# A Fourier stage whose sequence transform is split by parity and folded about the middle

## The chip, the cores and the metric

The kernel runs on one core of a Trainium2 chip. The metric is device time in microseconds (us) of one execution; the median over the runs shown is what is compared.

## What is computed

A two-layer transformer block in float32 on 512 tokens of 1024 features: a first block (projections, a bidirectional gated delta scan, a Fourier branch, gates, a mixture of 32 experts) and two plain attention layers. The change touches the Fourier branch alone. Of the projected input it takes 512 columns, in 4 groups of 128, and mixes each group over both axes:

```python
def fourier_mix(f):
    B, L, _ = f.shape
    fg = f.astype(jnp.float32).reshape(B, L, F_GROUPS, F_GROUP_DIM)
    return jnp.fft.fftn(fg, axes=(1, 3), norm='ortho').real.reshape(B, L, F_DIM).astype(f.dtype)
```

With f[l, d] for one group, the result at sequence position n and feature e is the sum over l and d of f[l, d] times (cos a cos b - sin a sin b), where a is the feature angle 2 pi d e / 128 and b the sequence angle 2 pi l n / 512. So it needs a cosine and a sine transform over the features, and then a cosine and a sine transform over the sequence, subtracted. The result is multiplied by `w_fourier_out` in the next stage.

## The kernel before

The program is a chain of stages. A stage opens a block with one instruction stream for each engine (TensorE, ScalarE, VectorE, GpSimd, and SyncE for the DMA queue); the streams wait for each other by semaphores, and each runs in its written order. All engines meet at a barrier at the end of a stage. PSUM is one tensor `g.PS` of 8 banks of 128 partitions x 512 floats.

`fourier_stage` (L1544 to L1640) is the stage that changes. The scan stage is ahead of it and the linear stage `ya` behind it, which multiplies the result by `w_fourier_out`. What each stream of the Fourier stage does, in order:

- **SyncE** loads the weights of the four groups (`W`, 512 KB each, L1565), the feature table `CS` (L1566: cosines and sines of 128 x 128), the sequence table `CL` (L1567: cosines and minus sines of 512 x 512, 2 MB), then the first pieces of the next stage's weights into a ring (L255) and some rows of biases (L1570), and waits for these rows.
- **TensorE** first projects: for each group 24 products of 128x512 with operands of the type fp32r (8 blocks of the contraction, each as hi x hi, lo x hi, hi x lo; the helper's lines L71 to L73), giving the group with features on partitions and 512 positions along the bank, in banks 0 to 3. Then the feature transform (L1586): for each pair of groups and each of four blocks of 128 positions, two plain float32 products of 128x256 (a block of positions as the stationary operand, `CS` as the moving one). Then the sequence transform (L1596): for each group, 8 plain float32 products of 128x512 that accumulate in one bank: 4 blocks of positions, cosine and sine. A plain float32 product is run as two passes, so the trace shows twice as many instructions as the code has products.
- **ScalarE** rounds the weights to the hi part (L1604), squares the scan's output `o` (L1608) and takes a root (L1610), both for a normalisation of `o` that has nothing to do with the transform, copies the projected groups out of PSUM to `fT` (L1614), copies half of the feature transform's results to `G` (L1617), and at last rounds each group's result to `FT.hi` (L1620). `G` lies in the memory of `W`.
- **VectorE** makes the low parts of the weights (L1626), sums the squares (L1629), inverts the root (L1631), scales `o` by it (L1634, four blocks), copies the other half of the feature transform (L1637), and makes `FT.lo` (L1640).

The order of the work is the written order of the streams; no planner is involved. Nothing is staggered across the groups: all four are projected, then all are transformed over the features, then all over the sequence. `ScalarE` and `VectorE` of the stage `ya` begin with the splits of its first weights (L646, L671), TensorE with its first product (L71).

`shape_tables` makes the tables on the host.

Of the kernel before, what the change touches and what calls it, by code (L numbers as in the profile page):

```python
# [15 lines left out]
P = 128  # L16
# [1526 lines left out]

def fourier_stage(nc, g, w_in, dft_feat, dft_seq, uT, FT, following, o, rows):  # L1544


    with Stage(nc, "fft", ["cs", "cl", "rows", "hi", "lo", "mm", "f", "g", "ga", "gd", "o", "oh", "sq", "ss", "rt", "rc"], [("w", NG)]) as st:
# [4 lines left out]
        CL = st.sb("CL", [P, NT, 2, SEQ])  # L1552
        fT = st.sb("fT", [P, NG, SEQ])
# [4 lines left out]
        G = W[:, :, :, :].rearrange("p g k n -> p (g k n)").rearrange("p (t g n) -> p t g n", t=NT, g=NG)  # L1558
        blk = st.block()

        @blk.sync
        def _(sp):
            wv = w_in.rearrange("(p k) n -> p k n", k=KD)
            for gr in range(NG):
                sp.dma_start(W[:, gr], wv[:, :, F_OFF + gr * P:F_OFF + (gr + 1) * P]).then_inc(s["w"][gr], 16)  # L1565
            sp.dma_start(CS[:, :], dft_feat).then_inc(s["cs"], 16)  # L1566
            sp.dma_start(CL[:, :, :, :], dft_seq.rearrange("(t p) c n -> p t c n", p=P)).then_inc(s["cl"], 16)  # L1567
            following.begin(sp, g.ring)
            for dst, src in rows:
                sp.dma_start(dst, src).then_inc(s["rows"], 16)  # L1570
            sp.wait_ge(s["rows"], 16 * len(rows))

        @blk.tensor
        def _(pe):
            for gr in range(NG):
                pe.wait_ge(s["lo"], gr + 1)
                for k in range(KD):
                    last = matmul3(nc, g.PS[:, gr, :], WP[:, gr, k, :], uT[:, k, :], k == 0, k == KD - 1)
                last.then_inc(s["mm"], 1)
            pe.wait_ge(s["cs"], 16)  # L1580
            for h in range(2):
                pe.wait_ge(s["f"], 2 * h + 2)
                for t in range(NT):
                    bank = (2, 3, 6, 7)[t] if h else (0, 1, 4, 5)[t]
                    for q in range(2):
                        last = nc.tensor.matmul(g.PS[:, bank, q * 256:(q + 1) * 256], fT[:, 2 * h + q, t * P:(t + 1) * P], CS[:, :], start=True, stop=True)  # L1586
                    last.then_inc(s["g"], 1)
            pe.wait_ge(s["cl"], 16)
            for gr in range(NG):
                if gr == 0:  # L1590
                    pe.wait_ge(s["ga"], NT)
                if gr == 2:
                    pe.wait_ge(s["gd"], NT)
                for t in range(NT):
                    for q in range(2):
                        last = nc.tensor.matmul(g.PS[:, gr, :], G[:, t, gr, q * P:(q + 1) * P], CL[:, t, q, :],  # L1596
                                                start=t == 0 and q == 0, stop=t == NT - 1 and q == 1)
                last.then_inc(s["o"], 1)

        @blk.scalar  # L1600
        def _(act):
            for gr in range(NG):
# [6 lines left out]
            act.wait_ge(s["ss"], NT)  # L1609
            nc.scalar.activation(rt[:, :, :], ss[:, :, :], ACT.Sqrt, bias=g.eps[:, 0:1], scale=1.0 / DH).then_inc(s["rt"], 1)  # L1610
            act.wait_ge(s["lo"], NG)
            for gr in range(NG):
                act.wait_ge(s["mm"], gr + 1)
                nc.scalar.copy(fT[:, gr, :], g.PS[:, gr, :]).then_inc(s["f"], 1)  # L1614
            for t in range(NT):
                act.wait_ge(s["g"], t + 1)
                nc.scalar.copy(G[:, t, 0:2, :], g.PS[:, (0, 1, 4, 5)[t], :].rearrange("p (g n) -> p g n", g=2)).then_inc(s["ga"], 1)  # L1617
            for gr in range(NG):
                act.wait_ge(s["o"], gr + 1)
                nc.scalar.copy(FT.hi[:, gr, :], g.PS[:, gr, :]).then_inc(s["oh"], 1)  # L1620

        @blk.vector
        def _(dve):
            for gr in range(NG):
                dve.wait_ge(s["hi"], gr + 1)
                nc.vector.tensor_tensor(WP.lo[:, gr], W[:, gr], WP.hi[:, gr].bitcast(F32), ALU.subtract).then_inc(s["lo"], 1)  # L1626
            for t in range(NT):
# [5 lines left out]
            for t in range(NT):  # L1633
                nc.vector.tensor_tensor(o[:, t], o[:, t], rc[:, t, :, None].to_broadcast([P, NV, DH]), ALU.mult)  # L1634
            for t in range(NT):
                dve.wait_ge(s["g"], NT + t + 1)
                nc.vector.tensor_copy(G[:, t, 2:4, :], g.PS[:, (2, 3, 6, 7)[t], :].rearrange("p (g n) -> p g n", g=2)).then_inc(s["gd"], 1)  # L1637
            for gr in range(NG):
                dve.wait_ge(s["oh"], gr + 1)
                nc.vector.tensor_tensor(FT.lo[:, gr, :], g.PS[:, gr, :], FT.hi[:, gr, :].bitcast(F32), ALU.subtract)  # L1640
# [97 lines left out]
def shape_tables():  # L1738
# [15 lines left out]
    j = np.arange(SEQ)  # L1754
    b = 2 * np.pi * ((j[:, None] * j[None, :]) % SEQ) / SEQ
    scale = 1.0 / np.sqrt(SEQ * P)
    seq = (np.stack([np.cos(b), -np.sin(b)], axis=1) * scale).astype(np.float32)
# [1550 lines left out]
```

## Time and profile before

| | us |
|---|---|
| median of 3 runs | 3851.17 (3850.42 to 3853.6) |
| profiled execution, its span from first to last instruction | 3851.9 |
| TensorE busy in it | 3515.4 (91%) |
| VectorE busy | 2738.6 (71%) |
| ScalarE busy | 1965.5 (51%) |
| GpSimd busy | 704.3 (18%) |

The profiled execution has no time of its own beside its span; the span is 0.7 us above the median of the runs. Engines overlap, so the busy times don't add up. The Fourier stage lies between about 704 and 771 us from the span's start. In the rows below, PE is TensorE's products, PEld its loads of stationary operands (they overlap PE), DVE VectorE, ACT ScalarE, POOL GpSimd. "128x512 f32" is partitions x elements; an idle time stands before the instruction that ended it, with the engine that released it. PEclk is the clock granted to TensorE, as a share of 2.4 GHz: 1.00 is 2.4 GHz, 0.50 is 1.2 GHz. Products are pipelined, so that the duration of one (592 ns) is longer than the distance between two starts.

### The profile page before, as it was taken

How to read it: one execution, taken by the hardware profiler on the slowest of the kernel's cores; microseconds unless marked ns; L12 is line 12 of the kernel's file. 1: busy time of each engine (PE TensorE's matmuls, PEld its weight loads, DVE VectorE, ACT ScalarE, POOL GpSimd, SP SyncE). 2: the span in 40 equal slices, each digit the busy share in tenths (PEclk: the TensorE clock that was granted, in tenths of full speed). 3: DMA queues.
4: the chain of work that ended last, by engine and by line, in shares of the span. 5: the costliest groups of instructions: out<-in, count | busy, mean ns of one | idle time of the engine just before them, and what ended most of it. 6: DMA issues, size and time to landing. Idle time of an engine off the chain costs nothing. (4 is left out here: it accounts for less than half of the span.)

```text
span 3851.9 us, 48477 instructions
## 1 busy us (share of the span) xinstructions
PE 3515.4 (91%) x17884; PEld 2912.3 (76%) x17884; DVE 2738.6 (71%) x3103; ACT 1965.5 (51%) x2530; POOL 704.3 (18%) x605
## 2 busy tenths in 40 slices
PE   4979999999969999999999997788899988879998
PEld 3768999677748888888888884667688767768876
DVE  5777777376569999999999996877676245753323
ACT  4533434223148888888888884357222223742222
POOL 1017767000000110011011012066000012720000
PEclk8989999999979999999999998899899989999999
DMA  5326011365359999999999995611466222013321
GB/s 171 113 109 242 12 45 34 111 228 186 133 227 356 377 376 390 377 374 390 378 374 390 379 374 215 199 32 45 131 197 196 88 79 54 34 46 103 93 93 66
DMA packets 285349, 752.62 MB, mean 195 GB/s; under 512 B 35528, under 2 KB 161160, under 8 KB 232186
## 3 DMA queue, kind: packets, MB, share of 16 engines
q1 hardware_dynamic: 271820, 696.01, 50.0%
q0 software_dynamic: 8480, 36.71, 2.7%
q10 hardware_dynamic: 4896, 17.83, 1.1%
q8 instruction: 101, 1.65, 0.2%
q14 instruction: 52, 0.43, 0.0%
HBM read 698.97 MB, written 57.01 MB: 196 GB/s over the span
## 5 line engine op out<-in xcount | busy, mean ns | idle before, releaser
L2238 DVE TENSOR_TENSOR ex_WP_lo<-ex_W,ex_WP_hi 128x2048 fp32r<-128x2048 f32 x408 | 918.5, 2285 | 43.9 <-ACT ex_WP_hi L2162 42.6
L2162 ACT CAST ex_WP_hi<-ex_W 128x2048 fp32r<-128x2048 f32 x408 | 766.9, 1910 | 196.9 <-PE PS L73 159.8
L71 PE MATMUL PS<-ex_WP_hi,ex_xT_hi 128*128 128x512 f32 x1056 | 418.7, 396 | 11.0 <-DVE ex_xT_lo L2247 5.6
L73 PE MATMUL PS<-ex_WP_hi,ex_xT_lo 128*128 128x512 f32 x1056 | 412.5, 391 | 0.0
L72 PE MATMUL PS<-ex_WP_lo,ex_xT_hi 128*128 128x512 f32 x1056 | 412.1, 390 | 0.0
L2080 POOL COPY r_idc<-r_idx 128x1 uint32 x33 | 73.9, 2241 | 1044.5 <-PE PS L2093 1044.5
L71 PEld LDWEIGHTS PS<-ex_WP_hi,ex_xT_hi 128*128 128x128 f32 x1056 | 198.9, 188 | 64.1 <-issue 24.8
L71 PE MATMUL PS<-ex_WP_hi,ex_aT_hi 128*128 128x512 f32 x576 | 230.0, 399 | 10.1 <-DVE ex_aT_lo L2247 5.3
L73 PEld LDWEIGHTS PS<-ex_WP_hi,ex_xT_lo 128*128 128x128 f32 x1056 | 198.7, 188 | 42.2
L72 PEld LDWEIGHTS PS<-ex_WP_lo,ex_xT_hi 128*128 128x128 f32 x1056 | 199.0, 188 | 39.4
L73 PE MATMUL PS<-ex_WP_hi,ex_aT_lo 128*128 128x512 f32 x576 | 226.4, 393 | 0.0
L72 PE MATMUL PS<-ex_WP_lo,ex_aT_hi 128*128 128x512 f32 x576 | 226.0, 392 | 0.0
L2743 POOL TENSOR_SCALAR lpj<-lpj 128x512 f32<-128x512 f32 (+2 forms) x128 | 176.2, 1387 | 50.5 <-DVE lpj L2905 50.1
L71 PE MATMUL PS<-lhT_hi,fu_WP_hi 128*128 128x512 f32 x464 | 181.7, 392 | 0.1
L73 PE MATMUL PS<-lhT_hi,fu_WP_lo 128*128 128x512 f32 x464 | 180.9, 390 | 0.0
L72 PE MATMUL PS<-lhT_lo,fu_WP_hi 128*128 128x512 f32 x464 | 180.7, 389 | 0.0
L3124 DVE TENSOR_TENSOR fd_WP_lo<-ringb,fd_WP_hi 128x1024 fp32r<-128x1024 f32 x44 | 53.6, 1225 | 169.4 <-ACT fd_WP_hi L3115 169.4
L1395 ACT COPY sc_Pm<-PS 128x512 f32<-128x512 f32 x144 | 84.4, 586 | 154.9 <-PE PS L1320 154.0
L71 PE MATMUL PS<-fd_WP_hi,lha_hi 128*128 128x512 f32 x352 | 139.2, 395 | 11.6 <-DVE fd_WP_lo L3124 11.6
L72 PE MATMUL PS<-fd_WP_lo,lha_hi 128*128 128x512 f32 x352 | 138.6, 394 | 0.0
L73 PE MATMUL PS<-fd_WP_hi,lha_lo 128*128 128x512 f32 x352 | 138.4, 393 | 0.0
L3115 ACT CAST fd_WP_hi<-ringb 128x1024 fp32r<-128x1024 f32 x44 | 45.7, 1048 | 176.1 <-PE PS L73 173.2
(623 smaller groups left out, 8637.4 us busy)
## 6 DMA issues: line engine op xcount, KB each, us to landing
ex_W<-in_w_gate SPq DMA_DIRECT2D x136, 1024.0 KB, 7.3
ex_W<-in_w_up SPq DMA_DIRECT2D x136, 1024.0 KB, 7.8
ex_W<-in_w_down SPq DMA_DIRECT2D x136, 1024.0 KB, 8.2
ringb<-in_w_gu SPq DMA_DIRECT2D x88, 512.0 KB, 4.1
ringb<-in_w_mod SPq DMA_DIRECT2D x72, 512.0 KB, 4.6
ringa<-in_w_mod SPq DMA_DIRECT2D x56, 512.0 KB, 4.8
s_ybuf<-x_sb SPq DMA_DIRECT2D x3, 8192.0 KB, 27.1
ringb<-in_w_down SPq DMA_DIRECT2D x44, 512.0 KB, 3.5
```

Of the source, the lines that this page charges most:

```text
L71: nc.tensor.matmul(out, lhs.hi, rhs.hi, start=start, stop=False)
L72: nc.tensor.matmul(out, lhs.hi, rhs.lo, start=False, stop=False)
L73: return nc.tensor.matmul(out, lhs.lo, rhs.hi, start=False, stop=stop)
L1395: nc.scalar.copy(Pm[:, b], PS4[:, 2 * b, :, :]).then_inc(s["pm"], 1)
L2080: nc.gpsimd.tensor_copy(r.idc[:, 0:1], r.idx[:, bass.ds(j + 2, 1)]).then_inc(s["icp"], 1)
L2162: nc.scalar.copy(WP.hi[:, c % RP], W[:, c % RAW]).then_inc(s["hi"], 1)
L2238: nc.vector.tensor_tensor(WP.lo[:, c % RP], W[:, c % RAW], WP.hi[:, c % RP].bitcast(F32), ALU.subtract).then_inc(s["lo"][c % RP], 1)
L2743: nc.gpsimd.tensor_scalar(score(n - 1), score(n - 1), rd[:, n - 1:n], None, ALU.mult).then_inc(s["na"], 1)
L3115: nc.scalar.copy(WP.hi[:, m % RP], ring.slot(m, stream.sources[m])).then_inc(s["hi"], 1)
L3124: nc.vector.tensor_tensor(WP.lo[:, m % RP], ring.slot(m, stream.sources[m]), WP.hi[:, m % RP].bitcast(F32), ALU.subtract).then_inc(s["done ...
```

## The change

The sequence transform uses two symmetries of cosine and sine. First, position n of the output is even or odd. For even n the angle repeats after 256 positions of the input, so the two halves of the input are added; for odd n it changes its sign, so they are subtracted. Second, each half (256 positions) is symmetric or antisymmetric about its middle, so that position m and 256 - m are added or subtracted. What is left are four arrays of 128 positions for each group (`SUM_COS`, `DIF_SIN`, `SUM_SIN`, `DIF_COS`) and four tables of 128 x 256. The input at the middle of the sum half (`QUARTER`) takes the place of row 0 of the sine tables, which is zero: it is brought there by a product with a tile `middle` (one column filled, the rest zero), and the tables' row 0 holds +-1 instead.

By engine:

- TensorE, for each group: the same 24 products of the projection; 5 plain float32 products of 128x128 for the features (L1586's 4 of 128x256 go); 4 of 128x256 for the sequence (L1596's 8 of 128x512 go). The groups are staggered: project 0, project 1, features 0, project 2, features 1, sequence 0, project 3, features 2, sequence 1, features 3, sequence 2, sequence 3.
- ScalarE: the copy of a projected group takes 256 columns instead of 512 (`upper`); a copy of 512 columns for each group behind the features (`gather`; four before on ScalarE and four on VectorE, now four on ScalarE); `high` writes `FT.hi` at every second element, since the bank holds the even positions and then the odd ones. The wait for `lo` now stands ahead of the root.
- VectorE, for each group: `folds`, with an addition and a subtraction of 256 elements (PSUM and `half`), a wait for both, an addition and a subtraction of 2 x 127 elements with one operand read backwards, and three copies of 2, 1 and 1 elements; then the scaling of one block of `o`. Two memsets stand ahead of the sums (128x4 and 128x512). `low` reads and writes at every second element.
- SyncE: `CL` is 512 KB instead of 2 MB.

```diff
@@ -1541,22 +1541,30 @@
                 nc.vector.tensor_copy(place(n), g.PS[:, n % 8, :].rearrange("p (j n) -> p j n", n=P)).then_inc(s["dve"], 1)
+HALF_SEQ, QUARTER = SEQ // 2, SEQ // 4
+
+
 def fourier_stage(nc, g, w_in, dft_feat, dft_seq, uT, FT, following, o, rows):
-    with Stage(nc, "fft", ["cs", "cl", "rows", "hi", "lo", "mm", "f", "g", "ga", "gd", "o", "oh", "sq", "ss", "rt", "rc"], [("w", NG)]) as st:
+    with Stage(nc, "fft", ["cs", "cl", "rows", "hi", "lo", "mm", "half", "sg", "zero", "fold", "g", "ga", "o", "oh", "sq", "ss", "rt", "rc"], [("w", NG)]) as st:
         s = st.s
         W = st.sb("W", [P, NG, KD, P])
         WP = pair(st.sb, "WP", [P, NG, KD, P])
         CS = st.sb("CS", [P, 2 * P])
-        CL = st.sb("CL", [P, NT, 2, SEQ])
-        fT = st.sb("fT", [P, NG, SEQ])
+        CL = st.sb("CL", [P, 4, HALF_SEQ])
+        half = st.sb("half", [P, NG, HALF_SEQ])
+        sg = st.sb("sg", [P, NG, 2, HALF_SEQ])
+        middle = st.sb("middle", [P, NG, P])
         sq = st.sb("sq", [P, 2, NV, DH])
         ss = st.sb("ss", [P, NT, NV])
         rt = st.sb("rt", [P, NT, NV])
         rc = st.sb("rc", [P, NT, NV])
-        G = W[:, :, :, :].rearrange("p g k n -> p (g k n)").rearrange("p (t g n) -> p t g n", t=NT, g=NG)
+        flat = W[:, :, :, :].rearrange("p g k n -> p (g k n)")
+        fold, G = [flat[:, n * NG * 4 * P:(n + 1) * NG * 4 * P].rearrange("p (g a n) -> p g a n", g=NG, a=4) for n in range(2)]
         blk = st.block()
+        SUM_COS, DIF_SIN, SUM_SIN, DIF_COS = range(4)
+        FEAT = {SUM_COS: slice(0, P), DIF_COS: slice(0, P), SUM_SIN: slice(P, 2 * P), DIF_SIN: slice(P, 2 * P)}
 
         @blk.sync
         def _(sp):
@@ -1564,7 +1572,7 @@
             for gr in range(NG):
                 sp.dma_start(W[:, gr], wv[:, :, F_OFF + gr * P:F_OFF + (gr + 1) * P]).then_inc(s["w"][gr], 16)
             sp.dma_start(CS[:, :], dft_feat).then_inc(s["cs"], 16)
-            sp.dma_start(CL[:, :, :, :], dft_seq.rearrange("(t p) c n -> p t c n", p=P)).then_inc(s["cl"], 16)
+            sp.dma_start(CL[:, :, :], dft_seq).then_inc(s["cl"], 16)
 ...
@@ -1572,33 +1580,58 @@
 
         @blk.tensor
         def _(pe):
-            for gr in range(NG):
+            def project(gr):
                 pe.wait_ge(s["lo"], gr + 1)
                 for k in range(KD):
                     last = matmul3(nc, g.PS[:, gr, :], WP[:, gr, k, :], uT[:, k, :], k == 0, k == KD - 1)
                 last.then_inc(s["mm"], 1)
-            pe.wait_ge(s["cs"], 16)
-            for h in range(2):
-                pe.wait_ge(s["f"], 2 * h + 2)
-                for t in range(NT):
-                    bank = (2, 3, 6, 7)[t] if h else (0, 1, 4, 5)[t]
-                    for q in range(2):
-                        last = nc.tensor.matmul(g.PS[:, bank, q * 256:(q + 1) * 256], fT[:, 2 * h + q, t * P:(t + 1) * P], CS[:, :], start=True, stop=True)
-                    last.then_inc(s["g"], 1)
-            pe.wait_ge(s["cl"], 16)
-            for gr in range(NG):
+
+            def features(gr):
+                pe.wait_ge(s["fold"], gr + 1)
                 if gr == 0:
-                    pe.wait_ge(s["ga"], NT)
-                if gr == 2:
-                    pe.wait_ge(s["gd"], NT)
-                for t in range(NT):
-                    for q in range(2):
-                        last = nc.tensor.matmul(g.PS[:, gr, :], G[:, t, gr, q * P:(q + 1) * P], CL[:, t, q, :],
-                                                start=t == 0 and q == 0, stop=t == NT - 1 and q == 1)
+                    pe.wait_ge(s["cs"], 16)
+                for a in range(4):
+                    out = g.PS[:, 4 + gr, a * P:(a + 1) * P]
+                    last = nc.tensor.matmul(out, fold[:, gr, a, :], CS[:, FEAT[a]], start=True, stop=a != SUM_SIN)
+                    if a == SUM_SIN:
+                        last = nc.tensor.matmul(out, middle[:, gr, :], CS[:, FEAT[SUM_COS]], start=False, stop=True)
+                last.then_inc(s["g"], 1)
+
+            def sequence(gr):
+                pe.wait_ge(s["ga"], gr + 1)
+                if gr == 0:
+                    pe.wait_ge(s["cl"], 16)
+                for parity, arrays in enumerate(((SUM_COS, SUM_SIN), (DIF_COS, DIF_SIN))):
+                    for n, a in enumerate(arrays):
+                        last = nc.tensor.matmul(g.PS[:, gr, parity * HALF_SEQ:(parity + 1) * HALF_SEQ], G[:, gr, a, :], CL[:, 2 * parity + n, :],
+                                                start=n == 0, stop=n == 1)
                 last.then_inc(s["o"], 1)
+            project(0)
+            project(1)
+            features(0)
+            project(2)
+            features(1)
+            sequence(0)
+            project(3)
+            features(2)
+            sequence(1)
+            features(3)
+            sequence(2)
+            sequence(3)
 
         @blk.scalar
         def _(act):
+            def upper(gr):
+                act.wait_ge(s["mm"], gr + 1)
+                nc.scalar.copy(half[:, gr, :], g.PS[:, gr, HALF_SEQ:SEQ]).then_inc(s["half"], 1)
+
+            def gather(gr):
+                act.wait_ge(s["g"], gr + 1)
+                nc.scalar.copy(G[:, gr], g.PS[:, 4 + gr, :].rearrange("p (a n) -> p a n", n=P)).then_inc(s["ga"], 1)
+
+            def high(gr):
+                act.wait_ge(s["o"], gr + 1)
+                nc.scalar.copy(FT.hi[:, gr, :].rearrange("p (m e) -> p e m", e=2), g.PS[:, gr, :].rearrange("p (e m) -> p e m", e=2)).then_inc(s["oh"], 1)
 ...
@@ -1607,37 +1640,59 @@
                     act.wait_ge(s["ss"], t - 1)
                 nc.scalar.activation(sq[:, t % 2], o[:, t], ACT.Square).then_inc(s["sq"], 1)
             act.wait_ge(s["ss"], NT)
+            act.wait_ge(s["lo"], NG)
             nc.scalar.activation(rt[:, :, :], ss[:, :, :], ACT.Sqrt, bias=g.eps[:, 0:1], scale=1.0 / DH).then_inc(s["rt"], 1)
-            act.wait_ge(s["lo"], NG)
-            for gr in range(NG):
-                act.wait_ge(s["mm"], gr + 1)
-                nc.scalar.copy(fT[:, gr, :], g.PS[:, gr, :]).then_inc(s["f"], 1)
-            for t in range(NT):
-                act.wait_ge(s["g"], t + 1)
-                nc.scalar.copy(G[:, t, 0:2, :], g.PS[:, (0, 1, 4, 5)[t], :].rearrange("p (g n) -> p g n", g=2)).then_inc(s["ga"], 1)
-            for gr in range(NG):
-                act.wait_ge(s["o"], gr + 1)
-                nc.scalar.copy(FT.hi[:, gr, :], g.PS[:, gr, :]).then_inc(s["oh"], 1)
+            upper(0)
+            upper(1)
+            gather(0)
+            upper(2)
+            gather(1)
+            high(0)
+            upper(3)
+            gather(2)
+            high(1)
+            gather(3)
+            high(2)
+            high(3)
 
         @blk.vector
         def _(dve):
+            def folds(gr):
+                dve.wait_ge(s["half"], gr + 1)
+                nc.vector.tensor_tensor(sg[:, gr, 0, :], g.PS[:, gr, 0:HALF_SEQ], half[:, gr, :], ALU.add).then_inc(s["sg"], 1)
+                nc.vector.tensor_tensor(sg[:, gr, 1, :], g.PS[:, gr, 0:HALF_SEQ], half[:, gr, :], ALU.subtract).then_inc(s["sg"], 1)
+                dve.wait_ge(s["sg"], 2 * gr + 2)
+                front, back = sg[:, gr, :, 1:P], sg[:, gr, :, HALF_SEQ - 1:P:-1]
+                nc.vector.tensor_tensor(fold[:, gr, 0:2, 1:P], front, back, ALU.add)
+                nc.vector.tensor_tensor(fold[:, gr, 2:4, 1:P], front, back, ALU.subtract)
+                nc.vector.tensor_copy(fold[:, gr, 0::3, 0], sg[:, gr, :, 0])
+                nc.vector.tensor_copy(middle[:, gr, 0:1], sg[:, gr, 0, QUARTER:QUARTER + 1])
+                nc.vector.tensor_copy(fold[:, gr, 1, 0:1], sg[:, gr, 1, QUARTER:QUARTER + 1]).then_inc(s["fold"], 1)
+
+            def low(gr):
+                dve.wait_ge(s["oh"], gr + 1)
+                nc.vector.tensor_tensor(FT.lo[:, gr, :].rearrange("p (m e) -> p e m", e=2), g.PS[:, gr, :].rearrange("p (e m) -> p e m", e=2),
+                                        FT.hi[:, gr, :].rearrange("p (m e) -> p e m", e=2).bitcast(F32), ALU.subtract)
             for gr in range(NG):
                 dve.wait_ge(s["hi"], gr + 1)
                 nc.vector.tensor_tensor(WP.lo[:, gr], W[:, gr], WP.hi[:, gr].bitcast(F32), ALU.subtract).then_inc(s["lo"], 1)
+            dve.wait_ge(s["lo"], NG)
+            nc.vector.memset(fold[:, :, SUM_SIN, 0:1], 0.0).then_inc(s["zero"], 1)
+            nc.vector.memset(middle[:, :, :], 0.0).then_inc(s["zero"], 1)
             for t in range(NT):
                 dve.wait_ge(s["sq"], t + 1)
                 nc.vector.reduce_sum(ss[:, t, :], sq[:, t % 2], AX.X).then_inc(s["ss"], 1)
             dve.wait_ge(s["rt"], 1)
             nc.vector.reciprocal(rc[:, :, :], rt[:, :, :]).then_inc(s["rc"], 1)
             dve.wait_ge(s["rc"], 1)
-            for t in range(NT):
-                nc.vector.tensor_tensor(o[:, t], o[:, t], rc[:, t, :, None].to_broadcast([P, NV, DH]), ALU.mult)
-            for t in range(NT):
-                dve.wait_ge(s["g"], NT + t + 1)
-                nc.vector.tensor_copy(G[:, t, 2:4, :], g.PS[:, (2, 3, 6, 7)[t], :].rearrange("p (g n) -> p g n", g=2)).then_inc(s["gd"], 1)
+            dve.wait_ge(s["zero"], 2)
             for gr in range(NG):
-                dve.wait_ge(s["oh"], gr + 1)
-                nc.vector.tensor_tensor(FT.lo[:, gr, :], g.PS[:, gr, :], FT.hi[:, gr, :].bitcast(F32), ALU.subtract)
+                folds(gr)
+                nc.vector.tensor_tensor(o[:, gr], o[:, gr], rc[:, gr, :, None].to_broadcast([P, NV, DH]), ALU.mult)
+                if gr == 3:
+                    low(0)
+            for gr in range(1, NG):
+                low(gr)
 def first_half(nc, g, I, C, scratch):
@@ -1751,10 +1806,14 @@
         selrow[r, r, :] = 1.0
     a = 2 * np.pi * ((i[:, None] * i[None, :]) % P) / P
     feat = np.concatenate([np.cos(a), np.sin(a)], axis=1).astype(np.float32)
-    j = np.arange(SEQ)
-    b = 2 * np.pi * ((j[:, None] * j[None, :]) % SEQ) / SEQ
+    m = np.arange(HALF_SEQ)
     scale = 1.0 / np.sqrt(SEQ * P)
-    seq = (np.stack([np.cos(b), -np.sin(b)], axis=1) * scale).astype(np.float32)
+    even = 2 * np.pi * ((2 * i[:, None] * m[None, :]) % SEQ) / SEQ
+    odd = 2 * np.pi * ((i[:, None] * (2 * m[None, :] + 1)) % SEQ) / SEQ
+    turns = 1.0 - 2.0 * (m % 2)
+    even_sin, odd_sin = -np.sin(even), -np.sin(odd)
+    even_sin[0], odd_sin[0] = turns, -turns
+    seq = (np.stack([np.cos(even), even_sin, np.cos(odd), odd_sin], axis=1) * scale).astype(np.float32)
     return {"t_ident": ident, "t_cum": cum, "t_levels": lev, "t_selrow": selrow, "t_dft_feat": feat, "t_dft_seq": seq}
 
 
```

## Rows read from the trace of the kernel before

**Rows 1.** the windows view (stretch: us, busy us of each engine with instructions, clock, DMA)

```profile
707.00:713.70 6.70, 2.65 (x6) 2.15 (x7) 2.77 (x3) 3.13 (x3) 0.00 (x0) 0.52 1.19 305
713.70:724.00 10.30, 10.30 (x45) 8.29 (x44) 9.29 (x9) 7.26 (x9) 0.00 (x0) 0.98 1.04 396
724.00:741.60 17.60, 17.60 (x80) 14.66 (x79) 4.27 (x6) 4.00 (x7) 0.00 (x0) 1.00 0.32 125
741.60:769.50 27.90, 27.83 (x66) 12.14 (x64) 2.99 (x5) 1.79 (x4) 0.00 (x0) 1.00 0.00 1
...
772.00:778.80 6.80, 4.90 (x12) 3.83 (x13) 5.47 (x4) 3.43 (x4) 3.33 (x2) 0.51 0.92 324
```

**Rows 2.** groups by line on TensorE, 703 to 790 (busy us, mean ns)

```profile
L1596 PE MATMUL PS<-fft_CL,fft_W 128*128 128x512 f32 x64 | 27.6, 592 | 0.0
...
L1586 PE MATMUL PS<-fft_CS,fft_fT 128*128 128x256 f32 x32 | 7.1, 379 | 0.0
```

**Rows 3.** the waits, 734 to 771.5 (us in total, times, longest)

```profile
ACT FT_hi L1620 <- PE PS L1596: 28.6, 4, 9.7
```

**Rows 4.** the timeline of ScalarE, 716 to 739 (start us, us, idle before)

```profile
721.06 0.32 ACT L1610 ACTIVATE fft_rt<-fft_ss,eps 128x32 f32<-128x32 f32 x1
...
723.89 0.59 ACT L1614 COPY fft_fT<-PS 128x512 f32<-128x512 f32 x1 [2.04 <-PE PS L73]
...
735.09 0.59 ACT L1614 COPY fft_fT<-PS 128x512 f32<-128x512 f32 x1 [5.01 <-PE PS L73]
735.96 0.59 ACT L1617 COPY fft_W<-PS 128x512 f32<-128x512 f32 x1 [0.28 <-PE PS L1586]
736.82 0.59 ACT L1617 COPY fft_W<-PS 128x512 f32<-128x512 f32 x1 [0.28 <-PE PS L1586]
```

**Rows 5.** the timeline of TensorE: last scan products, then the sequence products

```profile
698.66 1.06 PE L1371 MATMUL PS<-sc_T,ktok 128*128 128x128 f32 x8
...
741.80 27.63 PE L1596 MATMUL PS<-fft_CL,fft_W 128*128 128x512 f32 x64
```

**Rows 6.** the timeline of VectorE, 716 to 726.6

```profile
716.31 4.68 DVE L1629 TENSOR_REDUCE fft_ss<-fft_sq 128x8 f32<-128x1024 f32 x4
721.41 0.35 DVE L1631 RECIPROCAL fft_rc<-fft_rt 128x32 f32<-128x32 f32 x1 [0.41 <-ACT fft_rt L1610]
721.80 4.63 DVE L1634 TENSOR_TENSOR x_sb<-x_sb,fft_rc 128x1024 f32<-128x1024 f32 x4
```

**Rows 7.** the timeline at the stage's end and the next stage's start

```profile
769.47 0.59 ACT L1620 CAST FT_hi<-PS 128x512 fp32r<-128x512 f32 x1 [6.28 <-PE PS L1596]
770.08 0.69 DVE L1640 TENSOR_TENSOR FT_lo<-PS,FT_hi 128x512 fp32r<-128x512 f32 x1 [6.18 <-ACT FT_hi L1620]
...
773.90 0.80 PE L71 MATMUL PS<-ya_WP_hi,FT_hi 128*128 128x512 f32 x1 [4.47 <-DVE ya_WP_lo L671]
```

**Rows 8.** one line at a time (ns min/median/max): prices of small steps

```profile
L1434 DVE TENSOR_TENSOR sc_B<-sc_B,PS x32: 380/405/411, 436.2 to 652.4; 128x256 f32<-128x256 f32 x32
...
L1002 ACT COPY qkv_padc<-PS x16: 372/374/378, 90.7 to 244.8; 128x256 f32<-128x256 f32 x16
...
L2266 DVE MEMSET ex_bp<- x1: 912/912/912, 1101.0 to 1101.0; 128x1024 f32 x1
...
L2905 DVE RECIPROCAL lpj<-lpj x128: 148/158/165, 2562.5 to 3387.1; 128x1 f32<-128x1 f32 x128
```

**Rows 9.** the line L379, strided (yb) and unstrided (mo) reads

```profile
L379 DVE SCALAR_TENSOR_TENSOR yb_bacc<-ringa,silu,yb_bacc x7: 2112/2211/2293, 952.8 to 972.4; 128x1024 f32<-128x1024 f32 x7
L379 DVE SCALAR_TENSOR_TENSOR mo_bacc<-ringa,silu,mo_bacc x7: 1283/1284/1285, 1010.9 to 1029.4; 128x1024 f32<-128x1024 f32 x7
```

**Rows 10.** a TensorE wait in the scan, and the windows around it

```profile
606.25 1.53 PE L1298 MATMUL PS<-ident,sc_L 128*128 128x128 f32 x12 [1.64 <-DVE sc_L L1426]
...
606.00:609.50 3.50, 3.25 (x29) 3.25 (x30) 0.88 (x2) 0.00 (x0) 1.83 (x2) 1.00 0.00 0
609.50:620.00 10.50, 10.50 (x97) 10.50 (x96) 6.43 (x10) 4.40 (x8) 7.24 (x6) 1.00 0.01 2
```

## The prediction

> **What bounds the kernel now.** I read the windows view first, over the Fourier stage. From 713.7 to 769.5 us TensorE is busy all the time (10.30 of 10.30, 17.60 of 17.60, 27.83 of 27.90 us) while VectorE is busy 2.99 us of the last 27.90 and ScalarE less, and the DMA share there is 0.00 [rows 1]. Who works in that last stretch is told by the groups by line: 64 passes of L1596, the sequence transform, are the 27.6 us; the feature transform is 32 passes of L1586 [rows 2]. The waits show the other side: ScalarE waits 28.6 us in all for the four sequence results, and VectorE stands behind it [rows 3]. So what ends last is TensorE, and what it does longest is what the change cuts. The stage's exit is a chain of three: last product, the rounding of FT.hi (0.59 us), FT.lo (0.69 us), then the barrier and the next stage [rows 7].
>
> **What is removed.** The duration of a product includes its drain, so I use distances. 64 passes of 128x512 take 27.63 us and the last alone 0.59, so 63 distances are 27.04 us, 0.429 us each [rows 5]; 64 x 0.429 = 27.5 us. For 128x256, ScalarE's copies of feature results start 0.86 us apart (735.96 and 736.82) with four passes between them, 0.215 us each [rows 4]; 32 x 0.215 = 6.9 us. Together 34.4 us leave TensorE. The loads of stationary operands hide beside either, or the distance would not halve with the columns.
>
> **What is added on TensorE.** Features: 5 products x 2 passes x 4 groups = 40 passes of 128x128. In the scan, which has this size alone, 97 passes start in 10.50 us of unbroken work, 0.108 us each; and a run of twelve takes 1.53 us where a run of eight takes 1.06, 0.118 each [rows 5, 10]. I take 0.112: 40 x 0.112 = 4.5 us. Sequence: 4 x 2 x 4 = 32 passes of 128x256, 32 x 0.215 = 6.9 us. The projection keeps its 96 products; a group takes 5.60 us at full clock (ScalarE is released by group 1 at 723.89 and by group 3 at 735.09 [rows 4]). Net on TensorE: 34.4 - 11.4 = 23.0 us less.
>
> **Whether TensorE now waits.** The new order is worth following in time, since the folds stand on VectorE between a projection and its features.
>
> Group 0 is projected at about 723.85 - 5.60 = 718.25 us, group 1 at 723.85. But VectorE is late: the four sums run from 716.31 to 720.99, the root on ScalarE ends at 721.38, the reciprocal at 721.76 [rows 4, 6]. The two memsets come ahead of the sums. One of 1024 elements took 0.91 us [rows 8], so I take 0.5 us for 512, and 0.55 with the small one; the sums are back to back, so all behind them moves by 0.55: reciprocal done at 722.3. `upper(0)` stands behind the root on ScalarE, 721.85 to 722.2 (0.37 us for 256 columns [rows 8]). Folds(0) begin at 722.3: two operations of 256 elements at 0.40, two of 254 at the same, three tiny ones at 0.16 each (the one-element reciprocal took 158 ns) [rows 8], in all 2.1 us: 724.4. Features(0) could begin at 723.85, so there is a new wait of 0.6 us, 0.7 with the restart. Queued behind it on TensorE is project(2); nobody else waits. If the memsets cost nothing the wait is 0.1 us; if the folds take twice as long it is 2.8 us.
>
> From there, TensorE: features(0) to 725.7, project(2) 731.3, features(1) 732.4, sequence(0) 734.1, project(3) 739.7, features(2) 740.8, sequence(1) 742.6, features(3) 743.7, sequence(2) 745.4, sequence(3) 747.1. What each needs: fold(1) comes behind one scaling of `o` (1.22 us, 4.63 us for four [rows 6]) at 727.8, in time for 731.3; fold(2) at about 733.9 for 739.7; fold(3) is the tight one: upper(3) ends at 740.15, fold(3) at 742.3, 0.3 us before TensorE asks. Gather(3) (0.59 us for 512 columns [rows 4]) ends at 744.4, for 745.4. The four scalings, 4.6 us, fill VectorE's gaps; the scaling behind folds(3) holds low(0) to low(2), which still end before high(3). ScalarE has high(0) ahead of upper(3), but it ends at 734.8. So no second wait; the exit (0.59 + 0.69 us) is as before.
>
> **DMA.** `CL` moves 1.5 MB less and the pieces behind it land earlier. Worth nothing: in the trace of before the DMA share is 0.00 from 741.6 on and TensorE never waited for `CL` [rows 1]; the new stage's end (748.4) is still behind the last of the old traffic (0.32 share between 724 and 741.6, none after). The copies out of PSUM that VectorE loses (L1637) were off the path. The next stage's start, 3.1 us from FT.lo's end to its first product [rows 7], is the same work.
>
> **The sum.** -34.4 + 11.4 + 0.7 = -22.3 us. Against the profiled execution's own 3851.9 us that is 3829.6; against the median of the runs, 0.7 us lower, 3828.9. I put 3829.
>
> **Unknown prices.** (a) Writing and reading every second element. The nearest row is L379, which reads every eighth: 2.21 us against 1.28 for 1024 elements, 0.9 ns an element more [rows 9]. By it high(3) and low(3) would be 0.45 to 0.9 us longer each, 1.4 us in all; the other end is nothing. I take nothing: a step of two is far nearer to the row without a step than to the one with a step of eight. The Trainium skill's page "SBUF — State Buffer", section "Door 1: The DMA port swizzle", states that accesses within a 16-byte line run at full bandwidth, so that float32 may be strided up to 4 elements for free; by it the cost is zero, and L379's rows, beyond that step, agree. (b) The backward read. No row shows one. Below: 0.40 us as forward; above: L379's rate, 254 x 0.9 ns = 0.23 us more for each of two; a gain has no mechanism. I take 0.40. Both ends make fold(3) 0.45 us later, about its slack, and the first wait 0.45 us longer. (c) The memset, 0 to 0.9 us, taken 0.55. (d) TensorE's clock, as a rival.
>
> **Rivals.**
> 1. *VectorE becomes the bound of the tail.* If folds cost twice the 2.1 us (strides, drains at the wait within a fold), features(0) waits 2.1 us more and features(3) 1.8 us; with strided exits 1.4 us: 22.3 - 5.3 = 17 us, so 3834. For it: the slack at fold(3) is only 0.3 us. Against: the 256-element rows are tight, 380 to 411 ns.
> 2. *The clock dips once.* TensorE's clock falls to half after it stands still between stages (0.52 in 707 to 713.7, 0.51 in 772 to 778.8 [rows 1]). A dip of that length (6.8 us) at the new wait would cost half of it, 3.4 us: 3832. Against: in the scan TensorE waited 1.64 us, with 1.00 before, in and behind it [rows 10].
> 3. *Slower: the clock stays low.* The new order cycles through banks 0 to 7 with waits between short groups. If the clock fell to 1.2 GHz at features(0) and stayed there, the 22.6 us of TensorE work left in this stage would take 45.2, which by itself brings the time back to 3852; if it lasts through the next stage too, whose 96 products at 5.60/24 = 0.233 us are 22.4 us, another 19 us (3.4 us of them are paid in the dip that is there already) make it about 3871. It decides from the point where the low clock covers 30 us of work: 22.3 + 7.7. The Trainium skill's page "TensorE: Matmul & The Clock Gate", section "A second HAM failure mode: psum-queue depth-cycling", warns of just that: small idle times between groups of products while banks are cycled make the clock swing. The trace of before speaks against it: the scan runs small products with such waits at 1.00 [rows 10].
> 4. *The gain is not there*, since passes of 256 columns would be bound by their loads. But L1586's passes are of that very size with a load each, and are 0.215 us apart, half the distance of the 512-column ones; and the scan's 128-column passes, each with its load too, are half as far apart again [rows 4, 10]. Nearly excluded. Were each feature pass as far apart as one of 256 columns, 40 x 0.103 = 4.1 us would go: 3833.
>
> **How the numbers follow.** A measurement of this kernel can tell about 0.2%, 7.7 us, from no change. The forecast (3825 to 3831.5, that is its bounds and 2 us of scatter, about what the runs of before show) has 0.78; rival 1 has 0.11, rival 2 0.05, rival 4 0.02; rival 3 0.02, half of it ending near no change and half slower; something unnamed near no change 0.02. Faster needs under 3843.5: 0.96. Same 0.03, slower 0.01. The range: downwards no wait at all (3828.2) less scatter, and a low-clock stretch behind the stage that may fall otherwise against the shifted work (up to 3 us either way): 3824. Upwards it takes in rivals 1 and 2: 3836.
>
> **What would show it.** In the profile after: the stage's last FT.lo 22 us earlier, at about 748; sequence passes 32 of 128x256 and feature passes 40 of 128x128 with distances of 0.215 and 0.112 us; one wait of TensorE of 0.5 to 1 us for fold(0) and none for fold(3); clock 1.00 from 714 to the stage's end; everything behind shifted and otherwise the same. Wrong would be: a second wait for fold(3) or gather(3), a VectorE operation with a backward operand of 0.6 us or more, FT.hi of over 1 us, or a clock of 0.50 within the stage.

## The result and the profile after

| | before | after |
|---|---|---|
| median, us | 3851.32 (3850.42 to 3853.6, 4 runs) | 3828.68 (3826.51 to 3829.87, 4 runs) |
| profiled execution | 3851.9 | 3825.7 |
| first product of the Fourier stage to the end of its last FT.lo ("stage length") | 59.73 | 37.80 |

The ratio is 0.994 (95% interval 0.9927 to 0.9953): 22.6 us faster, where 3829 us and 22.3 us were forecast. The two profiled executions differ by 26.2 us, the stage by 21.9 of them. The rest isn't the change's as far as the profiles tell: 1.3 us of it lie ahead of the stage, and a second profile of the kernel before (below) is 2.8 us shorter than the first, which leaves 23.4. Where both the time and the span of one execution are known, the span is 1.8 to 2.3 us the shorter (3825.7 of 3827.75 after). So the execution profiled before took about 3854 us, an estimate, which is above the three runs of before. Its span of 3851.9 us should not be set beside their median, as the forecast and the part ahead of it do with the 0.7 us.

The windows view of the stage after, cut where the clock rises (stretch: us, busy us of TensorE, its loads, VectorE, ScalarE, GpSimd, clock, DMA):

```profile
709.73:715.10 5.37, 5.37 (x13) 4.21 (x14) 3.67 (x3) 3.87 (x5) 0.00 (x0) 0.50 1.11 346
715.10:747.53 32.43, 31.07 (x157) 26.09 (x155) 19.38 (x43) 10.58 (x17) 0.00 (x0) 1.00 0.29 111
```

In the second stretch TensorE is busy 31.07 of 32.43 us, and the 1.36 us left are about its exit, the time of FT.hi and FT.lo [rows 7]. So it is never stopped, and once the stage has begun the waits view shows no wait of TensorE in it. The clock was low for 5.37 us of the stage; before, for 3.0 us (711.04 to 714.0). At half clock that costs half its length. Without it the stage is 59.73 - 1.48 = 58.25 us before and 37.80 - 2.69 = 35.11 after: 23.1 us less, where the passes on TensorE were put at 23.0.

TensorE's timeline after, features(0), sequence(1), features(3), sequence(2) and (3):

```profile
723.45 0.83 PE L1595 MATMUL PS<-fft_CS,fft_W 128*128 128x128 f32 x6
...
739.70 1.89 PE L1606 MATMUL PS<-fft_CL,fft_W 128*128 128x256 f32 x8
741.43 0.83 PE L1595 MATMUL PS<-fft_CS,fft_W 128*128 128x128 f32 x6
742.10 0.39 PE L1597 MATMUL PS<-fft_CS,fft_middle 128*128 128x128 f32 x2
742.32 0.39 PE L1595 MATMUL PS<-fft_CS,fft_W 128*128 128x128 f32 x2
742.55 3.62 PE L1606 MATMUL PS<-fft_CL,fft_W 128*128 128x256 f32 x16
```

Features(0) has no idle time ahead of it. Features(3) and what follows give the distances: 741.43 to 742.55 for ten passes of 128x128, 0.112 us each, and 739.70 to 741.43 for eight of 128x256, 0.216 each. These are the rows that answer to [rows 5] and to the distances out of [rows 4].

VectorE's timeline after, from the second memset to the last tiny copy of folds(0), the last one of folds(3), and the last FT.lo:

```profile
715.27 0.48 DVE L1681 MEMSET fft_middle<- 128x512 f32 x1
715.67 4.63 DVE L1684 TENSOR_REDUCE fft_ss<-fft_sq 128x8 f32<-128x1024 f32 x4
720.71 0.35 DVE L1686 RECIPROCAL fft_rc<-fft_rt 128x32 f32<-128x32 f32 x1 [0.41 <-ACT fft_rt L1644]
721.10 0.42 DVE L1662 TENSOR_TENSOR fft_sg<-PS,fft_half 128x256 f32<-128x256 f32 x1
721.44 0.41 DVE L1663 TENSOR_TENSOR fft_sg<-PS,fft_half 128x256 f32<-128x256 f32 x1
721.89 0.42 DVE L1666 TENSOR_TENSOR fft_W<-fft_sg 128x254 f32<-128x254 f32 x1
722.23 0.42 DVE L1667 TENSOR_TENSOR fft_W<-fft_sg 128x254 f32<-128x254 f32 x1
722.57 0.16 DVE L1668 COPY fft_W<-fft_sg 128x2 f32<-128x2 f32 x1
...
722.70 0.14 DVE L1670 COPY fft_W<-fft_sg 128x1 f32<-128x1 f32 x1
...
740.79 0.14 DVE L1670 COPY fft_W<-fft_sg 128x1 f32<-128x1 f32 x1
...
746.84 0.69 DVE L1674 TENSOR_TENSOR FT_lo<-PS,FT_hi 128x512 fp32r<-128x512 f32 x1 [1.02 <-ACT FT_hi L1634]
```

The operations with a backward operand (L1666, L1667) take 0.42 us, as the forward ones (L1662) do. Operations issued back to back start 0.34 us apart, 0.45 where a wait for both sums lies between (L1663 to L1666), the tiny ones 0.07: folds(0) run from 721.10 to 722.84, 1.74 us. FT.lo with every second element takes 0.69 us, as in [rows 7].

ScalarE's timeline, a gather and the last two roundings:

```profile
739.90 0.59 ACT L1630 COPY fft_W<-PS 128x512 f32<-128x512 f32 x1 [0.74 <-PE PS L1595]
...
744.48 0.62 ACT L1634 CAST FT_hi<-PS 128x512 fp32r<-128x512 f32 x1 [1.14 <-PE PS L1606]
746.20 0.61 ACT L1634 CAST FT_hi<-PS 128x512 fp32r<-128x512 f32 x1 [1.11 <-PE PS L1606]
```

And TensorE's, the next stage's first product:

```profile
750.68 0.80 PE L71 MATMUL PS<-ya_WP_hi,FT_hi 128*128 128x512 f32 x1 [4.52 <-DVE ya_WP_lo L671]
```

FT.hi with every second element takes 0.61 to 0.64 us against 0.59 [rows 7]. The wait at the stage's exit is as before: 3.15 us from the end of FT.lo to the next product, against 3.13.

### The profile page after: what moved, and what is told of

Its sections match the earlier page's. It is cut to its first block and busy times, and to the rows that moved or that the text cites. A ratio compares the mean times of both kernels' runs of the same rounds, so it can differ in the third digit from the quotient of the medians.

```text
span 3825.7 us, 48456 instructions
## 1 busy us (share of the span) xinstructions
PE 3491.9 (91%) x17860; PEld 2906.4 (76%) x17860; DVE 2741.4 (72%) x3129; ACT 1965.4 (51%) x2530; POOL 703.6 (18%) x605
```

## Experiments

"Longer" and "shorter" are against the changed kernel, whose stage length is 37.80 us. Since medians scatter by 1 to 2 us, the stage length of the profile is named beside them.

**The changed kernel once more.**

> The changed kernel once more, as the measure for the three kernels beside it. The stage length (first product of the Fourier stage to the end of its last FT.lo) was 59.7 us before and 37.8 us after, where TensorE's clock was low for 10.2 us at the stage's start instead of 6.8. Theory (TensorE alone sets the stage): median 3827 to 3831, stage length 36.1 to 37.8 by how long the low clock lasts, TensorE's wait for fold(0) 0 to 0.5 us, larger where the clock rises early. Rival (the profile after was lucky, and the fold chain shows in other executions): a wait of TensorE of over 1 us.

Measured: 3827.9 us (5 runs; before 3850.95), stage length 37.83 us, no wait of TensorE. A third time, beside the last experiment: 3826.45 us and 37.82 us.

**Parity without folding.** In features, `sg` itself is stationary, in blocks of 128 positions; the table has the positions 0 to 255 for either parity, 1 MB. The features of a group go to one of two pairs of banks, so that those of groups 2 and 3 also wait for a gather.

```diff
-                    out = g.PS[:, 4 + gr, a * P:(a + 1) * P]
-                    last = nc.tensor.matmul(out, fold[:, gr, a, :], CS[:, FEAT[a]], start=True, stop=a != SUM_SIN)
...
+                    h, b = divmod(a, 2)
+                    last = nc.tensor.matmul(banks[:, gr % 2, a * 2 * P:(a + 1) * 2 * P], sg[:, gr, h, b * P:(b + 1) * P], CS[:, :], start=True, stop=True)
...
+                    for n in range(4):
+                        b, q = divmod(n, 2)
+                        last = nc.tensor.matmul(g.PS[:, gr, parity * HALF_SEQ:(parity + 1) * HALF_SEQ], G[:, gr, 2 * parity + b, q * P:(q + 1) * P],
+                                                CL[:, 4 * parity + n, :], start=n == 0, stop=n == 3)
```

> The split by parity without the folding about the middle: for each group 4 feature products of 128x256 instead of 5 of 128x128, and 8 sequence products of 128x256 instead of 4; VectorE has only the two operations of 256 elements, no memsets. The staggered order is kept. Theory (each pass costs its distance on TensorE): sequence 64 x 0.215 = 13.8, features 32 x 0.215 = 6.9, in all 20.7 us against 11.4, so 9.3 us longer than the changed kernel and 13.7 shorter than before: about 3838. Rival (the gain came from the staggering, or VectorE's folds bound the stage, so that their absence pays back the passes): within 3 us of the changed kernel.

Measured: 3838.98 us, ratio to before 0.9968 (0.9956 to 0.998); stage length 47.13 us, 9.3 longer, as forecast to the tenth. TensorE's timeline of it:

```profile
740.95 1.89 PE L1597 MATMUL PS<-fft_CS,fft_sg 128*128 128x256 f32 x8
742.68 3.62 PE L1607 MATMUL PS<-fft_CL,fft_W 128*128 128x256 f32 x16
746.13 1.89 PE L1597 MATMUL PS<-fft_CS,fft_sg 128*128 128x256 f32 x8
747.86 7.07 PE L1607 MATMUL PS<-fft_CL,fft_W 128*128 128x256 f32 x32
```

Eight feature passes, then sixteen sequence passes, all 0.216 us apart. So of the gain in passes the split by parity gives 13.7 us (58.25 less 44.48, the stage lengths before and here without the time lost at the low clock) and the folding 9.3, and VectorE's folds take nothing of it back.

**Not staggered.** TensorE runs `project` for the four groups, then `features`, then `sequence`; ScalarE `upper`, `gather`, `high` likewise.

```diff
-            project(0)
-            project(1)
-            features(0)
...
+            for step in (project, features, sequence):
+                for gr in range(NG):
+                    step(gr)
```

> All products of the changed kernel, but not staggered: project all four, features of all four, sequence of all four, and ScalarE's steps likewise. Theory (only the number of passes counts; three groups' features, 3.4 us, cover the 2.4 us of upper(3) and folds(3), and features(1) to (3) cover the gathers): within 0.5 us of the changed kernel, no wait of TensorE over 0.3 us. Rival (the staggering is what hides folds and gathers): 2.4 us or more longer, with a wait of TensorE ahead of features(3) or sequence(0).

Measured: 3827.58 us (ratio to before 0.9939, 0.9925 to 0.9952), stage length 37.97 us. TensorE's timeline:

```profile
735.61 0.83 PE L1595 MATMUL PS<-fft_CS,fft_W 128*128 128x128 f32 x6
...
740.07 7.07 PE L1606 MATMUL PS<-fft_CL,fft_W 128*128 128x256 f32 x32
```

From 735.61 on it never stops. The staggering as such is worth nothing. What matters is that other work of TensorE's lies between a group's projection and its features, and this order has that too.

**One group behind the other.** In this order nothing lies between. ScalarE takes `upper`, `gather`, `high` group by group too, and VectorE makes FT.lo of a group before the next group's folds.

```diff
-            project(0)
-            project(1)
-            features(0)
...
+            for gr in range(NG):
+                project(gr)
+                features(gr)
+                sequence(gr)
```

> All products of the changed kernel, one group wholly behind the other: project, features, sequence of group 0, then of group 1, and so on; nothing covers folds and gathers. Theory: TensorE waits for fold(0) about 4.9 us (it is done with group 0 at about 717.9, the fold at 722.8), for the three other folds 2.3 us each, for the four gathers 0.9 us each: 15.4 us longer than the changed kernel, plus 3.4 us for the clock, which falls at the first wait as it did at the wait of 3.57 us in the run with the scalings first; about 3847, and the shorter waits leave the clock at 1.00. Rival (the order of the groups is worth nothing, as the run without the stagger could be read): within 2 us of the changed kernel. Second rival (many short waits also lower the clock): over 3851.

Measured: 3853.55 us, ratio to before 1.0007 (0.9997 to 1.0016): the whole gain is gone. Stage length 61.88 us, 24.1 longer. The waits of TensorE in it (us in total, times, longest):

```profile
PE PS L1595 <- DVE fft_W L1654: 11.3, 4, 4.6
PE PS L1606 <- ACT fft_W L1622: 2.7, 4, 0.7
```

And the windows (columns as above):

```profile
724.20:731.00 6.80, 6.12 (x19) 5.14 (x20) 1.09 (x1) 0.61 (x2) 0.00 (x0) 0.53 0.22 86
731.00:737.00 6.00, 5.53 (x24) 4.13 (x22) 0.72 (x2) 0.98 (x2) 0.00 (x0) 1.00 0.00 0
...
741.00:745.00 4.00, 4.00 (x11) 3.23 (x12) 0.00 (x0) 0.48 (x1) 0.00 (x0) 0.60 0.00 0
745.00:751.00 6.00, 5.08 (x22) 3.76 (x20) 1.17 (x3) 0.52 (x2) 0.00 (x0) 1.00 0.00 0
751.00:758.00 7.00, 5.01 (x19) 4.11 (x20) 2.36 (x7) 0.59 (x1) 0.00 (x0) 0.76 0.00 0
```

The waits are 14.0 us, near the 15.4 expected. But the clock fell in each of the four groups: 0.53 over 6.8 us, then 0.60 over 4.0 and 0.76 over 7.0, and once more in the last. All low stretches in the stage behind its start sum to 17.0 us. TensorE works in 15.9 of them, which loses 8.0 us. 14.0 + 8.0 = 22.0 of 24.1. About 1.8 more are an estimate from the rows: a wait is counted from the end of the last product's duration (0.40 or 0.39 us), but the next product would have started 0.23 or 0.11 us behind its start, so each of the eight waits costs 0.17 or 0.28 us more than it is shown with. The first theory said that the short waits would leave the clock alone; that fell, and the second rival's mechanism holds. It is that of the slower rival of the prediction, but the clock swung and did not stay low: the Trainium skill's page "TensorE: Matmul & The Clock Gate", section "A second HAM failure mode: psum-queue depth-cycling", says that small idle times between groups of products make the clock swing. In this order the trace agrees, with 8.0 us lost. The changed kernel has no such idle times, so it neither bears this out nor speaks against it.

**All scalings first**, which moves fold(0) behind them:

```diff
             for gr in range(NG):
+                nc.vector.tensor_tensor(o[:, gr], o[:, gr], rc[:, gr, :, None].to_broadcast([P, NV, DH]), ALU.mult)
+            for gr in range(NG):
                 folds(gr)
-                nc.vector.tensor_tensor(o[:, gr], o[:, gr], rc[:, gr, :, None].to_broadcast([P, NV, DH]), ALU.mult)
...
```

> The changed kernel with VectorE's four scalings of o ahead of all folds, as their place was before. Fold(0) is ready 4.6 us later, fold(1) 3.5 us later. Theory: TensorE, 0.6 us of slack in the profile after, waits about 4 us for fold(0), and everything behind moves by that: 4 us longer than the changed kernel, if the clock stays at 1.00; if so long a stand makes the clock fall for about 6.8 us as at the stage ends, 7.4 us longer. Rival (slack elsewhere takes the wait in, since the later folds have 3 us and more to spare): under 1.5 us longer.

Measured: 3834.44 us, 6.5 longer than the changed kernel's 3827.9; stage length 44.28 us, 6.5 longer. TensorE's timeline at the wait:

```profile
727.97 1.65 PE L1595 MATMUL PS<-fft_CS,fft_W 128*128 128x128 f32 x6 [3.57 <-DVE fft_W L1670]
```

And the windows (columns as above):

```profile
728.00:733.00 5.00, 5.00 (x17) 4.42 (x18) 1.52 (x7) 0.58 (x1) 0.00 (x0) 0.50 0.00 0
733.00:755.00 22.00, 20.20 (x105) 17.10 (x103) 6.10 (x18) 4.96 (x9) 0.00 (x0) 1.00 0.00 0
```

A wait of 3.57 us, and 1.2 GHz from 726.4 to 733.2 us, 5.2 us of it under work. The wait is paid in full, and the clock adds half of these 5.2 us, 2.6: together 6.2 of the 6.5 us. None of the later slack takes it in.

**Two scalings first**, the same edit for two of the four.

> The changed kernel with two of the four scalings of o ahead of folds(0): fold(0) 2.3 us later. With the slack of 0.6 us TensorE waits about 1.7 us. Theory: the time grows by that alone and the clock stays at 1.00, as in the scan's wait of 1.64 us: 1.7 us longer than the changed kernel. Rival: this wait too is followed by a low clock of 6.8 us: 5.1 us longer.

Measured: stage length 39.63 us, 1.8 longer; 3828.5 us, which scatter hides. TensorE's waits:

```profile
PE PS L1595 <- DVE fft_W L1670: 1.4, 1, 1.4
```

And the windows (columns as above):

```profile
724.00:730.00 6.00, 4.56 (x26) 3.70 (x25) 3.25 (x15) 0.96 (x2) 0.00 (x0) 1.00 0.14 55
730.00:750.00 20.00, 18.54 (x98) 15.79 (x96) 8.27 (x20) 5.01 (x9) 0.00 (x0) 1.00 0.00 0
```

1.4 us of standing still cost about their own length (1.8 us of stage length in all), with the clock at 1.00.

**The wide table.** `CL` holds the table three times (1.5 MB).

```diff
-        CL = st.sb("CL", [P, 4, HALF_SEQ])
+        CL = st.sb("CL", [P, 3 * 4, HALF_SEQ])
```

> The changed kernel with the sequence table loaded three times over, 1.5 MB instead of 512 KB (the last two thirds are not read). Theory (the saved traffic is worth nothing): no difference over 0.5 us in the stage length (37.8 us), no wait of TensorE. Rival (the shorter load is part of the gain): 2 us or more longer, with a wait for the table or for the pieces of the next stage.

Measured: 3828.82 us, stage length 38.02 us, no wait of TensorE. The extra 1 MB, two thirds of the saved traffic, costs at most 0.2 us; the last third was not put back.

**The memsets on GpSimd**, behind its own wait for `lo`.

> The changed kernel with its two memsets on GpSimd, which is idle in this stage. The folds begin about 0.55 us earlier. Theory: TensorE has slack there already, so the stage length stays at 37.8 us. Rival (fold(0) is what TensorE is released by): 0.5 us shorter.

Measured: one time of 3827.0 us, stage length 37.81 us. The folds begin 0.5 us earlier behind the stage's first product (10.88 against 11.37 us), and features(0) begins 13.72 us behind it in both. Fold(0) is not what releases TensorE.

**The kernel before, once more.**

> The kernel before once more, for its profile: in all profiles of the new variants the clock was low for 10.2 us around the stage's start, in the one of before for 6.8 us. Theory (chance of where the low stretch begins): 6.8 or 10.2 us, stage length 59.7 or 60.6 us; the stage length less the time lost at the low clock agrees with the first within 0.2 us. Rival (the change itself makes the low stretch longer): 6.8 us again with 59.7 us.

Measured: one time of 3851.37 us, span 3849.1. The windows of the part of the low stretch that lies in the stage, and of the one behind the stage (columns as above):

```profile
709.30:714.60 5.30, 5.30 (x13) 4.14 (x14) 3.62 (x4) 3.80 (x5) 0.00 (x0) 0.50 1.11 358
...
772.70:776.10 3.40, 2.88 (x7) 2.30 (x8) 3.40 (x4) 2.05 (x3) 1.52 (x1) 0.50 1.02 397
```

The low stretch lasts from 704.4 to 714.6 us, 10.2 us, with a stage length of 60.79 us. Less half of the 5.3 us of it that lie in the stage that is 58.14, beside 58.25 of the first profile. So the longer low stretch isn't the change's. Behind the stage the clock was low for 3.4 us here, and for 6.8 us (772.1 to 778.9) in the first profile.

**A step further: the next stage's first piece split ahead.** The tables and copies that shrank leave room for a tile in which GpSimd splits the first piece of `w_fourier_out`. The code below is the new stream alone; the tile is also made ahead of the stage and handed to the next one.

```diff
+        @blk.gpsimd
+        def _(pool):
+            ahead.split(pool, g.ring, following, 0, s["ah"])
```

> The changed kernel, and GpSimd, idle in this stage, splits the first piece of the next stage's weights (hi and low part) into a tile kept for it; the memory is what the smaller tables and copies set free. The next stage's first product then need not wait for ScalarE and VectorE: 3.15 us from FT.lo's end to it become about 1.3 us. Theory: 1.9 us shorter than the changed kernel; if TensorE then stands too briefly for the clock to fall behind the stage (a wait of 1.4 us left it at 1.00, one of 2.2 and one of 0.7 close together did not), up to 3.4 us more: 3823 to 3827. Rival (the next stage is held by VectorE's splits of the pieces behind the first anyway): no gain over 0.5 us.

Measured: 3824.72 us (3822.43 to 3829.6), 3.2 below the changed kernel's 3827.9, on another chip and not beside it. The timeline, from the last FT.lo to the next product:

```profile
746.20 0.69 DVE L1678 TENSOR_TENSOR FT_lo<-PS,FT_hi 128x512 fp32r<-128x512 f32 x1 [1.02 <-ACT FT_hi L1634]
...
747.71 0.47 PE L71 MATMUL PS<-firsta_hi,FT_hi 128*128 128x512 f32 x1 [2.19 <-PEq L116]
```

And the windows (columns as above):

```profile
748.60:752.00 3.40, 3.40 (x10) 2.63 (x9) 3.23 (x3) 2.03 (x3) 0.00 (x0) 0.50 0.98 298
752.00:760.00 8.00, 8.00 (x36) 6.51 (x36) 1.64 (x3) 0.59 (x1) 3.44 (x2) 1.00 0.67 269
```

The product starts 0.82 us behind FT.lo instead of 3.15, so 2.3 us of standing still are won at that place. The low clock lasts 3.4 us instead of 6.8, another 1.7 us. But that part can't be put down to the edit: the kernel before once more and the kernel with two scalings first, both with the usual wait at the exit, had 3.4 us there as well. On the whole kernel the gain did not show side by side:

> The changed kernel, beside the next one, for a comparison on one chip: 3827 to 3829 us, stage length 37.8 us (36.1 if the low clock ends early).

> The version with the next stage's first piece split by GpSimd, once more. Theory: its profile was 4.4 us shorter (2.3 us of the wait behind the stage, 1.7 us by a low clock of 3.4 instead of 6.8 us), and the medians of two submissions 3.2 us apart; side by side it is 2 to 5 us shorter than the changed kernel. Rival (the difference was scatter): within 1 us.

Measured: 3826.45 us for the changed kernel, 3827.33 with the split ahead (3825.04 to 3829.0); profiled spans 3824.4 and 3825.3. The local gain is there again (0.82 us, and a low clock of 3.4 us against 6.8), and at the start of the experts' stage the kernel is still 1.6 us ahead (1123.6 against 1125.2 us), behind a Fourier stage that began 1.7 us later. That the kernel is 2 to 5 us shorter, as expected, was not borne out; whether it gains at all is open. The medians are 0.9 us apart with ranges of 4 us and more, and the scatter of low-clock stretches may hide it, which is argued and not shown.

## Why the prediction was right

- **The bound and the sum of passes** were right: 34.4 us of passes out, 11.4 in, at distances measured after as 0.216 and 0.112 us; 23.0 forecast, 23.1 found once the low clock is set aside. The profiles themselves differ by 21.9 in the stage, since the one after lost 1.2 us more there at the low clock. The run with the parity alone shows the same price per pass at an amount in between.
- **The new wait at features(0)** was wrong. 0.6 to 0.7 us were forecast and none came, for two reasons. The folds were put at 2.1 us by adding durations; back to back they took 1.74, so fold(0), though begun 0.1 us later than forecast, was ready 13.1 us behind the stage's first product (722.84 - 709.73), not 13.4. And TensorE came later than in the first profile, 13.7 instead of 12.8 us behind it, since its clock was low for longer. By the first profile's clock 0.3 us of the wait would be left. No profile of the changed kernel shows it, but each of them has the longer low stretch, so no run shows what happens with the shorter one.
- **The slack at fold(3)** was put at 0.3 us; it is 0.5 (740.93 to 741.43).
- **Unknown prices.** The memsets took 0.48 and 0.06 us, as taken. Reading backwards costs nothing here (0.42 us either way). Every second element costs 0.02 to 0.05 us on ScalarE and nothing on VectorE, so the upper bound from L379 [rows 9] was far off and the nearer row right. The Trainium skill's page "SBUF — State Buffer", section "Door 1: The DMA port swizzle", lets float32 be strided up to 4 elements for free. With a step of two the trace agrees on VectorE (0.69 us as before) and within 0.05 us on ScalarE.
- **DMA** at nothing was right as far as the wide table tests it, for 1 of the 1.5 MB.
- **The rivals** did not occur, none of the four. The mechanism of rivals 2 and 3 is real: a wait of 3.57 us cost 3.6 us and 2.6 more by the clock, and the serial order gave back everything. What kept it away is that the order puts work of other groups over each fold, which the prediction argued from slack of a few tenths. Even the wait of 0.7 us that it forecast would hardly have lowered the clock, since one of 1.4 us did not.
- **Chance.** The hit to a few tenths is luck: without the wait the sum is 3828.2, and single medians of this kernel lie between 3826.5 and 3828.7. Against the kernel before timed beside it, it was 22.6, 23.1 and 24.8 us faster in the three comparisons; the forecast wait made the sum 22.3 instead of 23.0.

## What to carry to other kernels

Where TensorE is busy without a gap, count the passes by the distance between their starts, and the gain of a cheaper formula comes out to a few tenths; preparing work on idle engines is free as long as something else of TensorE's lies over it. Follow the written order in time and look at each wait by itself: every one costs its own length, and a longer one costs a stretch at the low clock besides (here one of 1.4 us did not, those of 2.2 us and of 3.6 us did). The order need not be clever if it covers the steps: the simplest loop, with all of one step ahead of the next, was as good as the hand-made stagger.

## What was not expected of the hardware

- TensorE's clock stayed at 2.4 GHz behind a wait of 1.4 us, and fell to 1.2 GHz for 6.8 us behind one of 3.6 us. It fell for 3.4 us in the serial order, behind waits of 2.2 us with 1.1 us of products and another wait of 0.7 us behind them. The second wait isn't needed for it: with the split ahead TensorE waited once, 2.19 us, worked for 0.9 us, and then the clock fell for 3.4 us, in both runs. In the trace of before, on the other hand, two waits of 2.06 and 2.10 us (the products of 3250.54 and 2537.26 us) left it at 1.00. So the length of one wait doesn't settle it, and why is open.
- The low stretch around the stage's start was 6.8 us in the first profile of before and 10.2 us in all others, the second one of before among them: 1.1 us of that kernel's stage. Behind the stage it was 6.8 us in ten of the fourteen profiles and 3.4 us in four.
